# Expert weights fetched as pairs: 16384 B rows in 2 MiB tiles, eight places and one for the first, on a kernel of two transformer blocks

## The reference, cut to what matters

```python
def expert_choice_ffn(h, w_router, w_gate, w_up, w_down):
    cap = EC_CAPACITY * s // N_EXPERTS                        # 2 * 512 // 16 = 64
    affinity = jax.nn.softmax((h @ w_router), axis=-1)
    top_val, top_idx = lax.top_k(affinity.transpose(0, 2, 1), cap)
    xe = jax.vmap(lambda hb, ib: hb[ib])(h, top_idx)
    act = jax.nn.silu(einsum('becd,edf->becf', xe, w_gate)) * einsum('becd,edf->becf', xe, w_up)
    ye = einsum('becf,efd->becd', act, w_down) * top_val[..., None]
    # ye is added to the tokens it came from
```

## Time and profile before

| | |
|---|---|
| runs of the kernel before | 3399.21 us median of 3 (3398.0 to 3409.49) |
| profiled execution | 3399.32 us; its span 3397.5 us |
| PE busy | 2700.4 us, 79% of the span |
| DVE, ACT, POOL busy | 1632.4, 997.8, 699.3 us |
| granted TensorE clock over the span | 0.893 of full |
| transfers issued by SP (q1) | 522.87 MB |
| transfers issued by POOL (q0) | 543.20 MB |

### The profile page before, as it was taken

The page is one execution under the profiler, slowest core; times in us unless marked ns, Lnnn a source line. Parts: engine busy times, 40 slices in busy tenths (PEclk is TensorE's granted clock), DMA queues, the critical chain, the costliest instruction groups (busy, mean ns, idle before and its releaser), DMA issues.

```text
span 3397.5 us, 43961 instructions
## 1 busy us (share of the span) xinstructions
PE 2700.4 (79%) x17232; PEld 1384.2 (41%) x17232; DVE 1632.4 (48%) x3398; ACT 997.8 (29%) x2395; POOL 699.3 (21%) x603
## 2 busy tenths in 40 slices
PE   8798888785999999999997886787768755555555
PEld 6567566375333333333336763443324311111111
DVE  4745844764001010100107357667676577677764
ACT  2232233521000000000002335477444343344332
POOL 0411310000000000000000023334343344444442
PEclk9899899897999999999998898888878877877777
DMA  3211211145999999999994279999999999999997
GB/s 145 83 64 38 100 61 58 52 162 229 395 420 419 420 420 419 420 420 420 420 420 148 97 293 391 419 407 376 383 414 420 383 420 419 420 420 420 420 419 330
DMA packets 156190, 1068.86 MB, mean 315 GB/s; under 512 B 17360, under 2 KB 19280, under 8 KB 30544
## 3 DMA queue, kind: packets, MB, share of 16 engines
q0 software_dynamic: 75408, 543.20, 38.9%
q1 hardware_dynamic: 80576, 522.87, 38.1%
HBM read 1052.63 MB, written 13.37 MB: 314 GB/s over the span
## 4 chain that ended last, share of the span: by engine, by line
PE 52%; DMA 27%; DVE 13%; ACT 6%; issue 2%; POOL 1%; DVEq 0%; SPq 0%; ACTq 0%; POOLq 0%
PE ps L92 50%; DMA gb<-in_peer_uv,eidx 25%; DVE gb L146 2%; PE ps L97 2%; ACT L168 1%; ACT dots L168 1%; DMA ga<-in_ed 1%; DVE inv_x L115 1%; POOL gb L86 1%; ACT diag L168 1%; DVE expert_act L115 1%; DVE wa_lo L115 1%; ACT prob L168 0%; DVE rw_r L126 0%; DVE wa_hi L130 0%
## 5 line engine op out<-in xcount | busy, mean ns | idle before, releaser
L92 PE MATMUL ps<-gb,diag 64*64 64x512 f32 x4096 | 655.4, 763 | 443.8 <-ACT diag L168 429.1
L146 DVE CUSTOM_DVE_ANT_0 gb<-gb,xn 128x1024 f32<-128x1024 f32 x512 | 626.4, 1223 | 366.2 <-DMA gb<-in_peer_uv,eidx 366.0
L86 POOL DMA_INDIRECT gb<-in_peer_uv,eidx x512 | 563.0, 1100 | 989.5 <-PE ps L92 722.9
L92 PEld LDWEIGHTS ps<-gb,diag 64*64 64x64 f32 x4096 | 149.4, 157 | 880.5 <-ACT diag L168 768.0
L92 PE MATMUL ps<-ga,xt 128*64 128x512 f32 x1120 | 331.1, 600 | 2.5 <-DVE xt L120 2.5
L115 DVE TENSOR_TENSOR expert_act<-expert_act,ps 128x512 f32<-128x512 f32 x32 | 22.0, 687 | 539.7 <-PE ps L92 539.2
L168 ACT ACTIVATE dots<-dots 128x1 f32<-128x1 f32 (+1 forms) x374 | 75.9, 203 | 641.5 <-DVE dots L146 636.2
L115 DVE TENSOR_TENSOR x<-x,ps 128x512 f32<-128x512 f32 (+1 forms) x96 | 61.3, 643 | 366.6 <-PE ps L92 365.9
L168 ACT ACTIVATE diag<-cons,dots 128x128 f32<-128x128 f32 x512 | 205.5, 401 | 42.0 <-PE ps L92 0.4
L92 PEld LDWEIGHTS ps<-ga,xt 128*64 128x64 f32 x1120 | 118.9, 137 | 187.4 <-issue 180.1
L92 PE MATMUL ps<-h_hi,wa_hi 128*128 128x512 f32 x368 | 160.1, 435 | 34.3 <-DVE wa_lo L115 33.6
(11 more groups left out here) (331 smaller groups left out, 4011.3 us busy)
## 6 DMA issues: line engine op xcount, KB each, us to landing
ring<-in_wt SPq DMA_DIRECT2D x77, 1024.0 KB, 5.6
ga<-in_eg SPq DMA_DIRECT2D x70, 1024.0 KB, 26.1
ga<-in_eu SPq DMA_DIRECT2D x70, 1024.0 KB, 27.4
ga<-in_ed SPq DMA_DIRECT2D x68, 1024.0 KB, 27.7
gr<-in_eu SPq DMA_DIRECT2D x37, 1024.0 KB, 26.8
gr<-in_ed SPq DMA_DIRECT2D x34, 1024.0 KB, 27.6
ring<-in_eg SPq DMA_DIRECT2D x29, 1024.0 KB, 26.4
gr<-in_eg SPq DMA_DIRECT2D x29, 1024.0 KB, 27.0
```

The costliest lines, as they stand in the source:

```text
L86: self.e.indirect_dma_start(out, None, table, bass.IndirectOffsetOnAxis(ap=idx, axis=0)).then_inc(s, 16)
L92: i = self.e.matmul(out, l, r, start=st, stop=sp, skip_group_check=True)
L146: self.done(self.e.tensor_tensor_reduce(out=o, in0=a, in1=b, scale=scale, scalar=start, op0=o0, op1=o1, accum_out=acc), name)
```

## The change

The two tiles of a pair (the same part of expert 2c and of 2c + 1) become one tile of 2 MiB with rows of 16384 B; there are 192 tiles. The tiles have eight places of 2 MiB that are used in turn (`slots`), made of what were 16 places of 1 MiB or gaps, and a ninth, `GF`, that holds the first tile only. To make `GW` one unbroken region, `X` and `ring` trade places in SBUF and the ring's order is turned round; the small tensors of the router move to the end of A. Tile n > 8 waits for tile n - 8; tile 0 waits only for `mg_lo` (the operands of the output projection), tile 1 for the last small tiles in two of the ring's places. PE's matmuls and their order are the same; one in eight signals instead of one in four.

```diff
-O_COLS, O_SMALL, O_RING, O_X, D0, O_TAIL = 2696, 2792, 2984, 9128, 13224, 36824
+O_COLS, O_SMALL, O_X, O_RING, D0, O_TAIL = 2696, 2792, 2984, 7080, 13224, 36824
-    ring = [T(f"ring{i}", O_RING + 2048 * i, 2048) for i in range(NS)]
+    ring = [T(f"ring{i}", O_RING + 2048 * (NS - 1 - i), 2048) for i in range(NS)]
-    rt = A("router", 9216, 8, 16)
+    rt = A("router", 21760, 8, 16)
-    lgt, aff, top = A("logits", 9344, 4, 16), A("affinity", 9408, 512), A("top_val", 9920, 64)
+    lgt, aff, top = A("logits", 21888, 4, 16), A("affinity", 21952, 512), A("top_val", 22464, 64)
...
-    NE = 15
-    GA = [L(f"ga{i}", 2048 * i, 2048) for i in range(8)]
-    GR = [A(f"gr{i}", 2048 * i, 2048) for i in range(4)]
-    slots = GA + ring + GR
+    NE = 8
+    GA = [L(f"ga{i}", 4096 * i, 4096) for i in range(4)]
+    GW = [T(f"gw{i}", O_RING + 4096 * i, 4096) for i in range(4)]
+    slots = GW[0:1] + GA + GW[1:4]
+    GF = A("gf", 16640, 4096)
...
                     for k2 in range(4):
-                        for e2 in range(2):
-                            yield I[nm][2 * c + e2, fh, k2]
+                        yield I[nm][c, fh, k2]
             for f2 in range(8):
-                for e2 in range(2):
-                    yield I["ed"][2 * c + e2, f2]
+                yield I["ed"][c, f2]
+
+    def tile_place(n):
+        return slots[(n - 1) % NE] if n else GF
+
+    def of_expert(n, e2):
+        return tile_place(n).rearrange("p (e k c) -> p e k c", e=2, k=2)[:, e2, :, :]
 
     def sp_moe(sp):
         for n, src in enumerate(expert_tiles()):
-            s = n % NE
-            if n >= NE:
+            if n > NE:
                 sp.wait_ge(("moe", n - NE))
-            elif s < 8:
-                sp.wait_ge(("wo_ps", 3, 3), ("br", "lo", 7))
-            elif s < 11:
-                sp.wait_ge(("br", "lo", s - 3))
+            elif n == 0:
+                sp.wait_ge("mg_lo")
+            elif n == 1:
+                sp.wait_ge(("br", "lo", 6), ("br", "lo", 7))
+            elif n < 6:
+                sp.wait_ge(("wo_ps", 3, 3))
+            elif n == 6:
+                sp.wait_ge(("br", "lo", 5), "h_stored")
             else:
                 sp.wait_ge(("route_ps", 3), "h_stored")
-            sp.dma(slots[s], src, f"slot{s}", ("etile", n))
+            sp.dma(tile_place(n), src, f"slot{(n - 1) % NE if n else NE}", ("etile", n))
...
-                                          ("moe", n_) if (kk, n) == (1, 1) else None)
-                            n_ += 1
+                                          ("moe", n_) if (e2, kk, n) == (1, 1, 1) else None)
+                        n_ += 1
...
-            sp.wait_ge(("moe", (369, 370, 383)[s]))
+            sp.wait_ge(("moe", (185, 185, 190)[s]))
...
 def expert_in(w):
 
-    return w.reshape(16, 4, 2, 128, 2, 1024).transpose(0, 4, 1, 3, 2, 5).reshape(16, 2, 4, 128, 2048)
+    return w.reshape(8, 2, 4, 2, 128, 2, 1024).transpose(0, 5, 2, 4, 1, 3, 6).reshape(8, 2, 4, 128, 4096)
```

More of the change, by code:

```diff
@@ L1496, in ac_merge @@
                 ac_btile(ac, n + 6, 31 + n, "br")
-    lgt, aff, top = A("logits", 9344, 4, 16), A("affinity", 9408, 512), A("top_val", 9920, 64)
-    idxu, idxf = A("top_idx", 9984, 64, dt=U32), A("top_idx_f", 10048, 64)
-    tv8, ti8, ii8 = A("expert_val", 10112, 8), A("expert_idx_f", 10120, 8), A("expert_idx", 10128, 8, dt=I32)
-    two = A("two", 10144, 2, 128)
-    NE = 15
-    GA = [L(f"ga{i}", 2048 * i, 2048) for i in range(8)]
-    GR = [A(f"gr{i}", 2048 * i, 2048) for i in range(4)]
-    slots = GA + ring + GR
+    lgt, aff, top = A("logits", 21888, 4, 16), A("affinity", 21952, 512), A("top_val", 22464, 64)
+    idxu, idxf = A("top_idx", 22528, 64, dt=U32), A("top_idx_f", 22592, 64)
+    tv8, ti8, ii8 = A("expert_val", 22656, 8), A("expert_idx_f", 22664, 8), A("expert_idx", 22672, 8, dt=I32)
+    two = A("two", 22688, 2, 128)
+    NE = 8
[3 more added lines that the diff above has]
+    GF = A("gf", 16640, 4096)
     XE = [A(f"xe{i}", 10496 + 1024 * i, 1024) for i in range(2)]
@@ L1573, in pe_moe @@
                         for e2 in range(2):
-                            w = slots[n_ % NE].rearrange("p (k c) -> p k c", k=2)
+                            w = of_expert(n_, e2)
                             orow = slice(64 * e2, 64 * e2 + 64)
@@ L1604, in pe_moe @@
                             pe.mm(PS[DBK[n]][orow, :], AT[:, 2 * f2 + kk, orow], w[:, kk, 512 * n:512 * n + 512],
-                                  f2 + kk == 0, f2 == 7 and kk == 1, ("moe", n_) if (kk, n) == (1, 1) else None)
-                    n_ += 1
+                                  f2 + kk == 0, f2 == 7 and kk == 1, ("moe", n_) if (e2, kk, n) == (1, 1, 1) else None)
+                n_ += 1
             pe.mark(("down_ps", c))
@@ L1754, in sp_bias @@
         else:
-            sp.wait_ge(("moe", 383))
+            sp.wait_ge(("moe", 191))
         sp.dma(ab[h % 2], I["abias"][:, 512 * h:512 * h + 512], f"bias{h % 2}", ("bias", p, h))
@@ L1899, in square @@
             else:
-                ac.wait_ge(("moe", 383))
+                ac.wait_ge(("moe", 191))
             root(name, i, at)
@@ L2208, in block_program @@
     MIDDLE = [M(f"gb{6 + i}", o, 2048) for i, o in enumerate((10240, 12288, 16384))]
-    THIRD = T("gb9", O_RING + 2 * 2048, 2048)
-    LATE = [T(f"gb{10 + i}", O_RING + 2048 * i, 2048) for i in range(2)] + [M("gb12", 18432, 2048)]
+    THIRD = T("gb9", O_RING, 2048)
+    LATE = [T(f"gb{10 + i}", O_RING + 2048 * (NS - 1 - i), 2048) for i in range(2)] + [M("gb12", 18432, 2048)]
     STEPS, GROW, ADD_LAG = 27, 236, 2
@@ L2660, in layouts @@
         "eg": expert_in(f["w_exp_gate"][0]), "eu": expert_in(f["w_exp_up"][0]),
-        "ed": f["w_exp_down"][0].reshape(16, 8, 2, 128, 1024).transpose(0, 1, 3, 2, 4).reshape(16, 8, 128, 2048),
+        "ed": f["w_exp_down"][0].reshape(8, 2, 8, 2, 128, 1024).transpose(0, 2, 4, 1, 3, 5).reshape(8, 8, 128, 4096),
         "rows": np.concatenate([np.broadcast_to(v[None, :], (128, v.shape[0])) for v in
```

## The result

The changed kernel took 3389.35 us (median of 13 runs, 3383.08 to 3396.63) against 3401.91 us of the kernel before in the same sessions (13 runs, 3394.8 to 3416.5): ratio 0.9961, 95% interval 0.995 to 0.9972. The ratio makes it 13.3 us less (the two medians lie 12.6 us apart), with 14.5 forecast.

What follows compares the result with a forecast made beforehand. The prediction took the expert weight stream at 420 GB/s as the bound; -17.1 - 7.5 + 5.7 + 2.5 + 1.9 = -14.5 us from 3399.32 gave 3385 us. Forecast case 3376 to 3391 (0.68), whole range 3374 to 3400.

Steps and rivals of the forecast that it cites:

- What bounds the stage: Expert stage: the weight stream at 420 GB/s is the bound, 121.1 us a pair; PE has 13 us of slack.
- The rate, -17.1 at 428: Expert weight stream: 16384 B rows raise 420 GB/s to 428, so 366 MiB take 896.7 us instead of 913.8.
- The 422: GB/s in the bias table's window of 24576 B rows; evidence for the rival that the rate hardly moves, chance 0.14.
- an estimate of 6 us: Weight stream: halving the packets at 3 cycles each saves about 6 us over 366 MiB, making the sum about -3.
- Places, refill and tail: Expert stage: 18 MiB ready instead of 15, -7.5 us; later first refill, +5.7; coarser last tile, +1.9.
- The gather, +2.5: First pair's token rows, before PE's expert start: 16384 B neighbours lengthen it, moving PE's start by +2.5 us.
- turns: DMA engines alternate row by row between weights and gather: 8 rows an engine take 6.2 us instead of 3.7.
- Early tiles, 0: Tiles 0 and 1, fetched before the output projection ends, fill a queue full in any case: worth 0.
- moved tensors, 0: x and the small-tile ring trade homes, router tensors move: same instructions and operands, worth nothing.
- The signs: Expected trace times: PE's first expert matmul at 849, refill at 860, last down product's end about 1777 us.
- One bound: Upper end of the forecast case's 3376 to 3391 us, for 426 to 431 GB/s and gather 0 to 2.5 us.

Runs made afterwards that it cites:

- rows_8k: Changed kernel with each 2 MiB tile fetched as 256 rows of 8192 B instead of 128 of 16384 B; ratio 0.9998 to the kernel before.
- rows_4k: Changed kernel with each 2 MiB tile fetched as 512 rows of 4096 B; ratio 1.0075 to the kernel before.
- seven_places: Changed kernel with seven places used in turn instead of eight, the ninth still for tile 0; ratio 0.9951 to the kernel before.
- both_tail: Changed kernel with two tiles waiting for the first gather, tile 7 in the ninth place, last tile in two halves; 3377.49 us, ratio 0.9925.
- no_early: Changed kernel with tiles 0 and 1 also waiting for the end of the output projection; ratio 0.9964 to the kernel before.
- lone_seventh: Changed kernel with the ninth place holding tile 7, not tile 0, which is still fetched first; ratio 0.9957 to the kernel before.
- quiet_gather: Changed kernel with tiles 7 and 8 waiting until the first pair's gather has landed; ratio 0.9929 to the kernel before.

## Why the prediction was right

**What bounds the stage.** Right. The pairs moved from 121.1 to 118.7 us with the rate (50.9 / 0.427 is 119.2), and rows_8k takes the change's gain away alone.

**The rate, -17.1 at 428.** Right in mechanism and somewhat large: 427, 383.8 / 0.420 - 383.8 / 0.427 = 15.0 us, and 14.7 between rows_8k and the changed kernel. That 428 came so near is in part luck. It was the rate of one window of 14 us with 12288 B rows, and it was used for 16384 B without a step up; by the three lengths of rows_4k a 12288 B row takes some 463 ns, 425 GB/s (an estimate), so the window was high by about what the missing step was worth. The 422 that held the forecast down was no clean bound: of the 384 packets in that window 187 were under 2 KB, and not rows of the biases. By the Trainium skill's 3 cycles a packet ("DMA: Bandwidth & Descriptors", Why small descriptors are slow) the prediction had an estimate of 6 us; these runs don't agree with it, as three lengths show 8 to 10 ns a row.

**Places, refill and tail: -7.5 + 5.7 + 1.9 = +0.1.** Measured together, -1.0 (rows_8k against before, from the first matmul). One by one: the refill came 11.5 us behind PE's start instead of 5.4, +6.1; the 2 MiB of one place are 4.8 us (seven_places), which is the price per MiB that was used for three; the coarse tail is 2.1 (both_tail). With 3 MiB at that price these make +1.0, so 2 us of the -1.0 are not accounted for; two single executions stand behind it.

**The gather, +2.5.** PE's start moved by 1.9 us in the pair of profiles, by 1.7 and 2.3 in no_early and lone_seventh. The size is about right, but it was made from turns alone: beside 8192 B rows the gather loses 4.2 us against none (8.58 and 4.40), where the turns account for 2.5, so the term had more to give back than the prediction saw. That is what quiet_gather found; what the other 1.7 us are is open. The prediction also took the gather and the places as separate terms. seven_places shows that they are not: the tile that fills the eighth place is under way beside the gather, and the later start of PE takes back what the place is worth.

**Early tiles, 0; moved tensors, 0.** no_early shows the first. rows_8k has all the moves and is at 0.9998, so they cost nothing that shows.

**The signs.** With P at the forecast's 797.4, PE's first expert matmul is at 848.6 (849 forecast), the first refill at 860.05 (860) and the end of the last down product at 1777.6 (1777). The copy of h landed 23.9 us after its issue, and tiles 6 and 7 followed at P + 27.6 (P + 28.6). DMA stood idle in front of the refill for some 15 us by its busy share and for 16 by its rate, as forecast. One bound is not what its parts give: 426 GB/s with the gather at +2.5 is 3384.8 + 4.2 = 3389, not 3391.

The sum, -14.5, was -13.8 in the stage and -13.3 in the whole. Its parts missed by about 2 us or less each, and the misses partly cancel: the rate gave 2.1 less than forecast, the places 1.1 more, and the gather took 0.6 less. What no view of one execution could tell is the spread of P over ten microseconds, which is as large as the change.

## What to carry to other kernels

Where a stream of large transfers is the bound, price each row: here a row cost an engine 8 to 10 ns beside its bytes, so the rate was 1.7% higher at 16384 B than at 8192, and 2.6% lower at 4096 B. Longer rows made the small transfers beside them slower, so look for the one that the critical path waits for and keep the queue empty around it; that was worth 6 us of the stage here, but 2 us or less in the kernel before, where the stream had less idle time to give. A further place was worth its bytes over the rate at the first refill, if what fills it doesn't hold up something that the path waits for, and a place that is never refilled should hold the last tile that can be there, not the first.

## What the runs showed of the hardware that was not expected

The same gather of 128 rows of 4096 B took 4.4 to 4.7 us with no weights beside it and up to 11.26 us beside rows of 16384 B. And the same instructions ahead of the stage ended between 796.76 and 806.36 us in eleven profiled executions of kernels alike up to there but for the places of tensors and the two early tiles. The two latest, 803.62 and 806.36, show a granted clock of 0.92 from 200 to 600 us, the other nine 0.93 or 0.94; whether that is the cause is not shown.
